# A two-layer decoder trunk on one core: four chunks of the mixer's input projection multiplied as heads and rests, logits in pairs, and products for nobody in idle stretches

## The reference

```python
for l in range(2):                                   # x: (1, 512, 1024), float32 throughout
    h = rms_norm(x, norm_mix[l]); z = h @ w_in[l]    # one projection, split 12 ways
    (g_q, g_k, g_v, g_lr, g_r, d_q, d_k, d_v, i_q, i_k, i_w, c_u) = split(z)
    o_gla  = gated linear attention (4 heads, decays from g_lr), normed, times silu(g_r)
    o_dsa  = sparse attention: an indexer scores all earlier keys
             (sum over 8 heads of relu(i_q . i_k) * i_w), the 128 best per query stay,
             6 heads of softmax(rms_norm(d_q) . rms_norm(d_k) + bias) @ d_v
    o_conv = gated input, causal depthwise convolution of width 31, layer norm, silu
    x = x + concat(o_gla, o_dsa, o_conv) @ w_out[l]
    x = x + cross_attention(rms_norm(x), rms_norm(mem))      # 256 rows of memory
    x = x + moe(rms_norm(x))     # router picks 1 of 4 groups, 2 of its 4 experts per row:
                                 # silu(t @ w_gate[e]) * (t @ w_up[e]) @ w_down[e]
```

## Time and profile before

| | us |
|---|---|
| median of 3 runs (1676.96 to 1678.27) | 1678.24 |
| the profiled execution, whole | 1680.62 |
| its span, first to last instruction | 1678.7 |
| mean granted TensorE clock of it | 0.946 |

### The profile page before, as it was taken

The page is one execution under the profiler, slowest core; times in us unless marked ns, Lnnn a source line. Parts: engine busy times, 40 slices in busy tenths (PEclk is TensorE's granted clock), DMA queues, the critical chain, the costliest instruction groups (busy, mean ns, idle before and its releaser), DMA issues. The chain is left out here.

```text
span 1678.7 us, 18992 instructions
## 1 busy us (share of the span) xinstructions
PE 1543.9 (92%) x6170; PEld 1007.7 (60%) x6170; DVE 1169.2 (70%) x1728; ACT 819.7 (49%) x1226; POOL 426.1 (25%) x214
## 2 busy tenths in 40 slices
PE   7999989999876999999789999899998769999996
PEld 3444456545555888877534445565455558888774
DVE  3693478832257999999727933887323579999997
ACT  4422233441345788778454222234404458877882
POOL 0000113200002655554400001232000025666535
PEclk9999989999876999999889999899998779999999
DMA  7141301042115999999631420011330159999995
GB/s 244 57 100 45 130 1 51 28 151 85 66 51 171 372 399 400 397 399 399 230 116 38 101 65 11 1 51 55 124 112 39 51 191 387 400 398 398 399 400 215
DMA packets 150982, 307.40 MB, mean 183 GB/s; under 512 B 32982, under 2 KB 46204, under 8 KB 150796
## 3 DMA queue, kind: packets, MB, share of 16 engines
q1 hardware_dynamic: 139516, 265.10, 43.8%
q0 software_dynamic: 6912, 25.17, 4.0%
q10 hardware_dynamic: 4496, 16.40, 2.4%
HBM read 280.42 MB, written 27.40 MB: 183 GB/s over the span
## 5 line engine op out<-in xcount | busy, mean ns | idle before, releaser
L592 PE MATMUL ps<-hT,arena 128*128 128x512 f32 x672 | 307.2, 605 | 0.0
L1703 POOL TENSOR_TENSOR rest_w_down<-arena,head_w_down 128x2048 fp32r<-128x2048 f32 x30 | 195.0, 6499 | 186.5 <-ACT head_w_down L1847 186.5
L592 PEld LDWEIGHTS ps<-hT,arena 128*128 128x128 f32 x672 | 125.8, 194 | 150.6 <-issue 149.2
L1941 DVE TENSOR_TENSOR rest_w_down<-arena,head_w_down 128x2048 fp32r<-128x2048 f32 x30 | 154.7, 5156 | 11.1 <-ACT head_w_down L1847 11.1
L1941 DVE TENSOR_TENSOR rest_w_gate<-arena,head_w_gate 128x2048 fp32r<-128x2048 f32 x62 | 141.3, 2279 | 9.8 <-remote 9.5
L1941 DVE TENSOR_TENSOR rest_w_up<-arena,head_w_up 128x2048 fp32r<-128x2048 f32 x64 | 143.5, 2282 | 1.3 <-ACT head_w_up L1847 1.3
L1847 ACT ACTIVATE head_w_down<-arena 128x2048 fp32r<-128x2048 f32 x60 | 114.9, 1927 | 36.6 <-DMA arena<-in_w_down 36.5
L1847 ACT ACTIVATE head_w_gate<-arena 128x2048 fp32r<-128x2048 f32 x60 | 114.3, 1916 | 33.0 <-DMA arena<-in_w_gate 32.2
L1847 ACT ACTIVATE head_w_up<-arena 128x2048 fp32r<-128x2048 f32 x64 | 122.2, 1944 | 9.4 <-DMA arena<-in_w_up 9.3
L1747 PE MATMUL ps<-head_w_gate,xg_head 128*128 128x512 f32 x256 | 106.9, 417 | 15.8 <-DVE xg_rest L1947 15.1
L1001 DVE CUSTOM_DVE_ANT_0 scratch<-ps,scratch 128x128 f32<-128x128 f32 (+3 forms) x48 | 23.6, 491 | 129.0 <-PE ps L705 78.8
(11 more groups left out here) (316 smaller groups left out, 2944.6 us busy)
## 6 DMA issues: line engine op xcount, KB each, us to landing
arena<-in_w_gate SPq DMA_DIRECT2D x64, 1024.0 KB, 9.7
arena<-in_w_up SPq DMA_DIRECT2D x64, 1024.0 KB, 10.9
arena<-in_w_down SPq DMA_DIRECT2D x64, 1024.0 KB, 10.2
arena<-in_w_in SPq DMA_DIRECT2D x10, 1536.0 KB, 6.7
yrows<-yb ACTq DMA_DIRECT2D x30, 512.0 KB, 6.2
arena<-in_w_in SPq DMA_DIRECT2D x4, 2048.0 KB, 7.7
arena<-in_w_in SPq DMA_DIRECT2D x16, 256.0 KB, 4.9
yrows<-x SPq DMA_DIRECT2D x1, 4096.0 KB, 18.3
```

The lines of the kernel that those rows point to most:

```text
L592: last = nc.tensor.matmul(ps[n % 2][0:width, :], w[:, c, col:col + width], hT[:, c, :], start=(c == 0), stop=(c == KD - 1))
L1703: nc.gpsimd.tensor_tensor(wl[2][:, c, :], raw[2][:, c, :], wh[2][:, c, :].bitcast(F32), ALU.subtract)\
L1941: nc.vector.tensor_tensor(wl[q][:, c, :], raw[q][:, c, :], wh[q][:, c, :].bitcast(F32), ALU.subtract)\
```

## The change

Seven parts; line numbers of the kernel after are not those of the rows.

1. **Heads and rests.** Chunks 2 to 5 (`dq`, `dk`, `dv`, `gq` and `gk`: 14 jobs a layer) are multiplied in three fp32r products instead of one in float32. ACT copies `hT` into `hT_head` (128x4096) and each chunk into `w_head`, POOL subtracts into `hT_rest` and `w_rest` (in the chunk's own slot).
2. **x kept in memory.** `hT_head` lies where x lies. In layer 0 x is read again from the input; in layer 1 SP writes it to `xrows` at the end of layer 0, and ACT waits for that (`s_kept`). x comes back after the last job ahead of the steps, and the additions of block 2 wait for it (`s_xt`). Two other DMAs are moved or read another source: the filling of `yrows`, and `heads`.
3. **Logits in pairs.** In even steps those of n + 2 and n + 3, in odd steps none.
4. **Products for nobody.** `idle_products(n)` issues n float32 products of 128x512 of ones into a free bank: 2 after each of the four turns of rows at the start, 3 behind the router's products, 3 and 8 further on in the router, 2 + 2 + 2 at the turns between the layers.
5. `gate_up` waits for each half of the rows' rests apart.
6. POOL's MEMSET of `AT` (128x2048) stands in step 1 instead of at the start.
7. Semaphores are merged or renamed (`factors_done`, `sum_done`).

```diff
+        hT_head = nc.alloc_sbuf_tensor_at("hT_head", [P, KD, S], F32R, offset=x_at)
+        def idle_products(n):
+            for _ in range(n):
+                nc.tensor.matmul(ps[7], ones[:, :], ones[:, 0:1].to_broadcast([P, 512]), start=True, stop=True)
...
+                    sp.wait_ge(sN["proj_done"], BEFORE_STEPS)
+                    for t in range(NT):
+                        rows = xrows[P * t:P * t + P, :] if l else A["x"][0, P * t:P * t + P, :]
+                        sp.dma_start(x[:, t, :], rows).then_inc(s_xt[t], 16)
...
                             row_turned(pe, t)
+                            idle_products(2)
...
+                    def split_project(n):
+                        chunk, col, width, kind, name, i = JOBS[n]
+                        m = SPLIT.index(chunk)
+                        pe.wait_ge(sN["heads_in"], m + 2)
+                        pe.wait_ge(sN["rests_in"], m + 2)
+                        wh, wl = w_head[m % 2], w_rest[k_of(chunk)]
+                        for c in range(KD):
+                            if kind == "T":
+                                o, at = ps[n % 2][0:width, :], slice(col, col + width)
+                                pairs = ((wh[:, c, at], hT_head[:, c, :]), (wl[:, c, at], hT_head[:, c, :]), (wh[:, c, at], hT_rest[:, c, :]))
...
-                        if n + 2 < NS:
+                        if n % 2 == 0 and n + 2 < NS:
                             logits(n + 2)
+                            logits(n + 3)
...
+                    def rows_head():
+                        act.wait_ge(sN["rows_hT"], NT)
+                        act.wait_ge(sN["rows_hA"], NT)
+                        if l:
+                            act.wait_ge(s_kept, 16 * NT)
+                        nc.scalar.activation(hT_head[:, :, :], hT[:, :, :], ACT.Copy).then_inc(sN["heads_in"], 1)
+                    def chunk_head(m):
+                        chunk, w = SPLIT[m], LOADED[SPLIT[m]]
+                        act.wait_ge(s_w[k_of(chunk)], chunks_loaded(chunk))
+                        if m == 1:
+                            act.wait_ge(sN["dots_done"], len(DOTS))
+                        if m >= 2:
+                            act.wait_ge(sN["proj_done"], done(("dq", "dk")[m - 2]))
+                        nc.scalar.activation(w_head[m % 2][:, :, 0:w], chunk_at(chunk)[:, :, 0:w], ACT.Copy).then_inc(sN["heads_in"], 1)
+                    rows_head()
+                    chunk_head(0)
                     act.wait_ge(sN["proj_done"], 1)
...
+                    chunk_head(1)
                     for n in range(6):
                         evacuate(AFTER_IDX + n)
...
+                        if n == 2:
+                            chunk_head(2)
+                    chunk_head(3)
...
                 def _(gp):
-                    do(nc.gpsimd.memset(AT, 0.0), "at_zero")
+                    def chunk_rest(m):
+                        gp.wait_ge(sN["heads_in"], m + 2)
+                        k, w = k_of(SPLIT[m]), LOADED[SPLIT[m]]
+                        nc.gpsimd.tensor_tensor(w_rest[k][:, :, 0:w], chunk_at(SPLIT[m])[:, :, 0:w], w_head[m % 2][:, :, 0:w].bitcast(F32),
+                                                ALU.subtract).then_inc(sN["rests_in"], 1)
...
                     route(3)
+                    idle_products(3)
...
                     last.then_inc(sN["r_sums"], 1)
+                    idle_products(3)
...
                     last.then_inc(sN["r_sums"], 1)
+                    idle_products(8)
...
+                        if q == 0:
+                            dve.wait_ge(s_xt[t], 16 * (l + 2))
...
+                        for t in range(NT):
+                            sp.wait_ge(s_add, summed(l, LAST, t))
+                            sp.dma_start(xrows[P * t:P * t + P, :], x[:, t, :]).then_inc(s_kept, 16)
...
                     def gate_up(n):
-                        pe.wait_ge(sN["blk_xl"], 2 * n)
+                        def halves_in(q, j):
+                            pe.wait_ge(sN["blk_xl"], 2 * n - 1 + j)
+                            pe.wait_ge(*split(q, j, n))
...
                     if l + 1 < L:
+                        idle_products(2)
                         row_turned(pe, 2)
+                        idle_products(2)
                         row_turned(pe, 3)
+                        idle_products(2)
```

More of the change, by code:

```diff
@@ L273, in program @@
         hT = lay("hT", [P, KD, S])
+        place_of_mixg = place[0]
         mixg = lay("mixg", [P, GH, S])
@@ L298, in program @@
         up = 3 * SLOT
+        SPLIT = [2, 3, 4, 5]
+        hT_head = nc.alloc_sbuf_tensor_at("hT_head", [P, KD, S], F32R, offset=x_at)
+        hT_rest = nc.alloc_sbuf_tensor_at("hT_rest", [P, KD, S], F32R, offset=slots_at + 4 * (up + 3072))
+        w_head = [nc.alloc_sbuf_tensor_at(f"w_head{i}", [P, KD, 512], F32R, offset=at)
+                  for i, at in enumerate((slots_at + 4 * (up + 7168), place_of_mixg))]
+        w_rest = [nc.alloc_sbuf_tensor_at(f"w_rest{i}", [P, KD, 512], F32R, offset=slots_at + 4 * SLOT * i) for i in range(NSLOT)]
         ya = [[view(arena, at + D * t, D) for t in range(NT)] for at in (2 * SLOT, up + SLOT)]
@@ L460, in program, with k_of, chunks_loaded @@
             NJ = len(JOBS)
+            def k_of(chunk):
+                return chunk % NSLOT
+            def chunks_loaded(chunk):
+                return 16 * sum(len(CHUNKS[c]) for c in range(k_of(chunk), chunk + 1, NSLOT))
             def done(name):
@@ L577, in _ @@
                             row_turned(pe, t)
+                            idle_products(2)
                     pe.wait_ge(sN["rows_hT"], NT)
                     pe.wait_ge(sN["rows_hA"], NT)
+                    def split_project(n):
[8 more added lines that the diff above has]
+                                pairs = ((wh[:, c, at], hT_head[:, c, :]), (wl[:, c, at], hT_head[:, c, :]), (wh[:, c, at], hT_rest[:, c, :]))
+                            else:
+                                o, at, tile = ps[n % 2][:, 0:width], slice(col, col + width), slice(P * i, P * i + P)
+                                pairs = ((hT_head[:, c, tile], wh[:, c, at]), (hT_head[:, c, tile], wl[:, c, at]), (hT_rest[:, c, tile], wh[:, c, at]))
+                            for a, (lhs, rhs) in enumerate(pairs):
+                                last = nc.tensor.matmul(o, lhs, rhs, start=(c == 0 and a == 0), stop=(c == KD - 1 and a == 2))
+                        last.then_inc(sN["proj_done"], 1)
                     def project(n, chunks=range(KD)):
@@ L589, in project @@
                         w = chunk_at(chunk)
+                        if chunk in SPLIT:
+                            split_project(n)
+                            return
                         for c in chunks:
@@ L793, in evacuate @@
                         act.wait_ge(sN["proj_done"], n + 1)
-                        if name == "gq" and i == 0:
-                            act.wait_ge(sN["at_zero"], 1)
                         if kind == "o":
@@ L1122, in _ @@
                                                    channel_multiplier=1), "causal_done")
+                    for m in range(1, len(SPLIT)):
+                        chunk_rest(m)
                     def level_keys(v):
@@ L1391, in head_squares @@
                         if n >= 2:
-                            act.wait_ge(sN["cn_sum"], n - 1)
-                        do(nc.scalar.activation(sq[:, n % 2, :], src, ACT.Square), "cn_sq", wait=False)
+                            act.wait_ge(sN["sum_done"], NORMS + n - 1)
+                        do(nc.scalar.activation(sq[:, n % 2, :], src, ACT.Square), "sq_ready", wait=False)
                     for n in range(3):
@@ L1402, in _ @@
                         act.wait_ge(ca_, lns - 2 + n)
-                        do(nc.scalar.activation(wide[n], wide[n], ACT.Exp, scale=-0.5), "cn_root", wait=False)
+                        do(nc.scalar.activation(wide[n], wide[n], ACT.Exp, scale=-0.5), "sums_root", wait=False)
                     act.wait_ge(sN["cp_done"], 4)
```

48 lines of the change are left out of this document (30 added, 18 removed).

## The result

| | before | after |
|---|---|---|
| median | 1677.60 us | 1612.05 us |
| lowest and highest of 4 | 1675.45, 1678.27 | 1608.62, 1616.00 |
| span of the profiled execution | 1678.7 | 1608.8 |
| mean granted clock | 0.946 | 0.968 |

The ratio is 0.9612, 95% interval 0.9587 to 0.9637: 3.9% faster. Forecast were 1626 to 1627, in a range of 1608 to 1650. The executions of after lie 7 us apart where those of before lie 3 apart; why, the experiments show.

The account below looks back on a forecast made before the run. PE was taken as the bound, alone ahead of the steps, with DVE near in them. Layer 0 21.4, between layers 3.85 and layer 1 26.7 sum to 52.0 us: 1626 to 1627, range 1608 to 1650.

Parts of the forecast that it names:

- the split: Jobs ahead of the steps: three fp32r products instead of one float32 gain 17.8 us a layer, bounds 17.1 and 18.7.
- the closing TENSOR_SCALARs: DVE operations closing each top-k tile; POOL's third and fourth rests would start 1 us behind two of them, no collision taken.
- rival 2: Top-k: POOL's rests collide with DVE's closing TENSOR_SCALARs, stalls of about 7 and 9 us, 1648 us; chance 0.10.
- rival 4: Top-k and norms: POOL's rests hold DVE back in every operation, slower, 1701 us or 1685; chance 0.03.
- rival 5: Jobs ahead of the steps: split products start 0.29 apart and give no speedup, 36 us less gain, 1662; chance 0.03.
- The steps: Logits in pairs gain 6 us a layer, between 2 and 9; at most 8.1 by PE's time alone.
- rival 1: Steps: DVE becomes the bound and the pairs give nothing, 12 us less gain, 1639; chance 0.15.
- The start: Layer 0: eight products of ones between the turns delay everything behind by 5.3 us, bounds 3.3 and 7.
- Router and experts: Warm sums, half waits and warm first gate products, less a possible delay: 2.9 us a layer, between -5 and +5.
- rival 3: Router: products for nobody delay the barrier, 5 us a layer behind instead of 2.9 ahead, 1643 us; chance 0.14.
- The even chance of gate products at the upper level: Experts' start: warm first gate products would save 2.8 us; at an even chance counted as 1.4.
- Between the layers: Filled gaps keep the clock up: turns 0.8 + 0.4 and job 0 2.65, together 3.85 us, bounds 0 and 5.

Follow-up runs that it names:

- e9: after with logits one head at a time, and products of ones ahead of the turns of step 6 (2) and step 7 (4); 1624.16 us, ratio 0.9689.
- e8: after with 2 products of ones ahead of the turn of step 6 and 4 ahead of that of step 7; 1611.06 us, ratio 0.9601.
- e6: before with 4 products of ones ahead of the turn of step 7 in each layer; 1669.22 us, ratio 0.9956.
- e7: after with 2 products of ones ahead of the turn of step 6 only; 1622.72 us, ratio 0.9669.
- e1: after with logits one head at a time again, all else kept; 1634.06 us, ratio to before 0.9741.
- e2: after without the eight products of ones at the start of layer 0; 1613.74 us, ratio 0.9619.
- e3: after without any product for nobody (start, router, between the layers); 1618.53 us, ratio 0.9631.
- e4: after with each block's first gate product waiting for all the rests of the rows, not a half; 1622.79 us, ratio 0.9668.
- e11: after with products of ones ahead of steps 0, 6, 7 and 18, and six instead of eight at the router's end; 1610.26 us, ratio 0.9590.
- e5: before with logits in pairs and nothing else changed; 1662.77 us, ratio 0.9907.

## Why the prediction was right, and where a size was off

**What bounds it, and the split: right.** 17.8 a layer forecast, 18.0 twice measured, from the spacing of the experts' products; the head and rest times, the order in which they come ready and the distance of 1 us to the closing TENSOR_SCALARs came as computed. Rivals 2, 4 and 5 did not occur. For rival 2 the margin was real but thin, 1.0 and 0.5 us, and no run here moved a rest onto a closing, so its price stays untested.

**The steps: the term that was mis-sized**, "I take 6, between 2 and 9". Measured 14.0 and 11.4. The pairs' own worth was near the forecast, 4.6 a layer by the steps' lengths and 6.5 by the medians (e9 against e8), and rival 1 did not occur. The Trainium skill's rule on row groups ("TensorE: Matmul & The Clock Gate", Part 3), which by itself would make the saving the full 8.1, is not contradicted: PE's own saving is 7.3, and some 3 of it go into longer waits for DVE. The rest of the 25.4, 12 to 16 us, is where the lower clock lay, and that step of the forecast left it out though it is in the very row it used: "where it is late PE stands idle (4.15 at 231.55) and saving on PE gives nothing". It counted the idle time and not the step behind it, which PE did at the lower level in 12.5 us instead of 6.8. I took that stretch to be fixed. e6 removes it without any other part of the change, e7 puts it back, e1 and e9 show it with single logits.

How pairs move it is shown in part. With them PE comes to the turn of step 6 earlier and waits 1.82 to 1.92 there instead of 1.33 to 1.43, and in the layers with a short step 7 the lower clock lay in step 6. e7, which fills that wait, has a long step 7 in both layers. But the wait alone does not decide: it was 1.82 too in layer 0 of e2, e3 and e4, where the clock stayed up through step 6 and step 7 was long. With pairs and nothing filled, 6 of 10 layers were short, with single logits none of 4. So that after's profile has both layers short is in part luck; the spread of its executions, 7 us, is wide enough for a long step 7 in one layer.

**The start: -2.9 instead of -5.3.** About 1.0 of the 2.4 is the execution: two products at the lower level took 2.4 in after's profile and not 3.4, but 3.4 in e8 and e11, as forecast. 1.1 is my reading: I counted the turns by their rows' lengths, 1.94 and 1.16, where they are 1.73 and 0.87 apart from what follows. The 0.3 of gaps did not come.

**Router and experts: 4.4 and 1.8 for 2.9 each.** In both layers the half waits gave 1.0. Up to the turns of the experts' rows layer 0 gained nothing: the sums end 1.7 earlier against the end of the steps, but the eight products end when the barrier opens and hold it some 1.6, rival 3 in small. The even chance of gate products at the upper level came out well in layer 0 only; in layer 1 the clock fell behind the third, and eight of them were 0.43 apart, 1.6 us. Against the end of the steps, layer 1's first gate product comes 2.4 earlier, the last product of the experts 2.9, and the end 1.8, where layer 0 has 1.1 and 4.4 for the first two. Its eight products took 8.63 instead of 9.57, so the turns behind them come 1.3 earlier; why the part behind its last expert product is 1.1 longer than before stays open.

**Between the layers: 5.1 for 3.85.** Job 0 gave the 2.65 forecast and the turns 1.35 for 1.2. The other 1.1 lies ahead of the first product for nobody: PE waits 4.18 for DVE's rows there where it waited 5.68. What shortened that wait stays open: it was 4.45 to 6.08 in the kernels without products for nobody and 3.88 to 4.29 in most with them, but 5.64 in e11 and 5.79 in e7.

The terms' errors add up: 13.4 from the steps, 2.4 from the start, 1.2 from the boundary, 0.5 from the experts, 0.4 from the split: 17.9 of a total gain of 69.8. The time stayed inside the range because that was wide enough for them.

## What to carry to other kernels

A wait of TensorE can cost twice when the clock falls with it: once the wait, which another engine sets, and once the next stretch at half the speed, if that one is bound by TensorE. So read, beside the engine that bounds a step, the granted clock of the step behind each wait of some us. Products of ones in the wait cost little as long as they end before the awaited signal. Which waits to fill depends on what follows: filling the one ahead of the step that TensorE bounds gained 8.4 us (e6), filling only the one before it lost 10.7 (e7), as the fall moved to the next. And where an execution can fall on either side, compare step lengths in several profiles before giving an edit the credit.

## What the runs showed of the hardware

- The granted clock fell within a wait of 4.14 to 4.24 us in every profile that had one at step 7 (before, e1, e2, e3, e4, e5 in layer 1, e7; in before at 229.96, 1.6 us ahead of the turn) and stayed low through the step, and it stood at 1.00 in all twelve layers where products filled it.
- Behind shorter waits it went both ways: behind 2.27 us ahead of step 0 the step took 7.66 in some layers and 9.2 in others; behind 2.41 us the gate products ran at full speed in layer 0 of after and at half in its layer 1.
- It also fell with no wait over 0.3 us in the 12 us before: at 182.17 in before, behind 16 products of 128x2 and two of logits.
- At the start the upper level came between 11.49 and 16.99 us in the fourteen profiles: 11.49 to 14.73 with products of ones between the turns, 12.25 to 16.99 without.
- POOL's subtraction of 128x3072 took 6.83 and of 128x4096 9.05, 2.2 ns an element of each partition, beside DVE's MAX8 and MATCH_REPLACE; in the experts, beside DVE's subtractions, 3.2.
